# Layers written out one by one in a two-layer transformer step, with the seam between them ordered by token tile

## The reference, cut to what matters

```
for l in range(DEPTH):
    mod = silu(c) @ w_ada[l] + b_ada[l]             # sh1, sc1, g1, sh2, sc2, g2
    u = rmsnorm(h, norm1_g[l]) * (1 + sc1) + sh1
    proj = u @ w_in[l]                              # q, k, v, conv input, gates
    merged = sigmoid(gate_a) * attention_branch + sigmoid(gate_c) * conv_branch
    h = h + g1 * (merged @ w_out[l])
    u2 = rmsnorm(h, norm2_g[l]) * (1 + sc2) + sh2
    h = h + g2 * grouped_moe(u2)                    # 16 experts, two for each token
y = rmsnorm(h, final_norm_g)
```

## Time and profile before

| | us |
|---|---|
| median of 3 runs | 1873.3 (1868.39 to 1873.57) |
| profiled execution, its own time | 1872.31 |
| its span | 1870.7 |
| PE busy | 1565.5 (84%) |
| DVE busy | 1221.8 (65%) |
| ACT busy | 785.7 (42%) |
| POOL busy | 738.5 (39%) |

### The profile page before, as it was taken

The page is one execution under the profiler, slowest core; times in us unless marked ns, Lnnn a source line. Parts: engine busy times, 40 slices in busy tenths (PEclk is TensorE's granted clock), DMA queues, the critical chain, the costliest instruction groups (busy, mean ns, idle before and its releaser), DMA issues.

```text
span 1870.7 us, 27095 instructions
## 1 busy us (share of the span) xinstructions
PE 1565.5 (84%) x8954; PEld 1338.9 (72%) x8954; DVE 1221.8 (65%) x1662; ACT 785.7 (42%) x1178; POOL 738.5 (39%) x440
## 2 busy tenths in 40 slices
PE   2699899989998975999549989998999988499970
PEld 0589766679997764777438986666999967377750
DVE  0658588878937364777194947887886445477725
ACT  0422577752224132766142247776222413176621
POOL 2124399421114201887212329862111220179941
PEclk7799999999999976999869999999999989599995
DMA  7612165322212642999852205551222262479976
GB/s 289 200 45 68 53 208 203 99 58 80 68 57 91 247 156 110 342 356 338 314 187 74 68 30 181 188 163 36 68 69 78 80 247 83 178 281 353 379 268 235
DMA packets 131206, 310.06 MB, mean 166 GB/s; under 512 B 11636, under 2 KB 81396, under 8 KB 109984
## 3 DMA queue, kind: packets, MB, share of 16 engines
q1 hardware_dynamic: 104096, 224.41, 35.0%
q0 software_dynamic: 16400, 42.90, 6.1%
q10 hardware_dynamic: 10560, 40.90, 5.7%
HBM read 287.06 MB, written 39.44 MB: 175 GB/s over the span
## 4 chain that ended last, share of the span: by engine, by line
PE 62%; DMA 14%; DVE 11%; issue 7%; ACT 4%; POOL 1%; DVEq 0%; ACTq 0%; POOLq 0%; SPq 0%
PE ps L539 26%; PE ps L498 9%; PE ps L800 6%; PE ps L597 3%; PE ps L607 2%; DVE gu_lo L1498 2%; DMA raw_x<-in_w_down 2%; PE ps L454 2%; DMA raw<-in_w_down 2%; PE ps L866 2%; DMA raw<-in_w_up 2%; PE ps L586 2%; DMA raw<-in_w_ada 2%; PE ps L846 2%; PE ps L587 1%
## 5 line engine op out<-in xcount | busy, mean ns | idle before, releaser
L2279 POOL TENSOR_TENSOR w_lo<-raw,w_hi 128x1024 fp32r<-128x1024 f32 (+1 forms) x46 | 162.5, 3535 | 554.9 <-ACT w_hi L1106 554.9
L539 PE MATMUL ps<-u_hi,w_hi 128*128 128x320 f32 x768 | 238.9, 311 | 5.4 <-ACT probs L1205 5.4
L539 PE MATMUL ps<-u_lo,w_hi 128*128 128x320 f32 x768 | 238.1, 310 | 0.0
L539 PE MATMUL ps<-u_hi,w_lo 128*128 128x320 f32 x768 | 238.1, 310 | 0.0
L1106 ACT ACTIVATE w_hi<-raw 128x2048 fp32r<-128x2048 f32 (+1 forms) x64 | 101.3, 1591 | 293.7 <-PE ps L539 133.9
L1853 DVE SCALAR_TENSOR_TENSOR glu<-glu,convw 128x670 f32<-128x670 f32 x164 | 171.1, 1043 | 6.1 <-DVE o_lo L1808 0.6
L539 PEld LDWEIGHTS ps<-u_hi,w_hi 128*128 128x128 f32 x768 | 144.8, 189 | 6.0 <-ACT probs L1205 5.9
L539 PEld LDWEIGHTS ps<-u_lo,w_hi 128*128 128x128 f32 x768 | 144.8, 189 | 0.1
L539 PEld LDWEIGHTS ps<-u_hi,w_lo 128*128 128x128 f32 x768 | 144.8, 189 | 0.0
L2384 POOL DMA_INDIRECT xe<-u_d,tab_u x34 | 68.4, 2012 | 179.6 <-issue 145.2
L1713 DVE TENSOR_TENSOR pt_lo<-ps,pt_hi 128x512 fp32r<-128x512 f32 x160 | 109.7, 687 | 29.9 <-ACT pt_hi L1231 27.8
(11 more groups left out here) (379 smaller groups left out, 4254.2 us busy)
## 6 DMA issues: line engine op xcount, KB each, us to landing
raw<-in_w_ada SPq DMA_DIRECT2D x52, 1024.0 KB, 5.1
raw<-in_w_in SPq DMA_DIRECT2D x48, 512.0 KB, 5.0
raw_x<-in_w_gate SPq DMA_DIRECT2D x16, 1024.0 KB, 7.0
raw<-in_w_up SPq DMA_DIRECT2D x16, 1024.0 KB, 8.3
raw_x<-in_w_down SPq DMA_DIRECT2D x16, 1024.0 KB, 9.2
raw_x<-in_w_up SPq DMA_DIRECT2D x14, 1024.0 KB, 8.6
raw<-in_w_gate SPq DMA_DIRECT2D x14, 1024.0 KB, 6.5
raw<-in_w_down SPq DMA_DIRECT2D x14, 1024.0 KB, 9.2
```

Of the source, the lines that this page charges most:

```text
L539: ins = mm(ps[:, b, 0:HALF], (w_hi, w_lo)[w][:, s, cols(k):cols(k) + P], xs[x][:, k, half * HALF:(half + 1) * HALF], start=(k == 0 and w + ...
L2279: g_.tensor_tensor(w_lo[:, n % 2, 0:k], raw[:, n % 2, 0:k], w_hi[:, n % 2, 0:k].bitcast(F32), ALU.subtract).then_inc(*G.up("g_lo", "w_lo", n))
```

## The change

The five loops over layers become Python loops: each layer's instructions are written out, and every wait compares with a constant. What differs between the layers can then be left out of one of them.

- The results of layer 0 move to the head of layer 1. ACT issues the first three reads of `y_in` (`results_in`) in place of the five, and the other two from inside `squares`. DVE makes the result of tile t+1 (`result_before`) ahead of `u_lo_of(t)` and `um_of(t + 1)`, and `w_lo` of units 0 and 1 behind `um_of(0)` and `um_of(1)`; those of units 2 and 3 come after the last tile.
- ACT runs `squares(0)`, `squares(1)`, and then for each t `u_hi_of(t)`, `squares(t + 2)`, `q_of(0, t - 1)`. The squares write their unused output into `y_in`.
- PE transposes tile t+1 between the two halves of the projection of tile t.
- Each store of `h` has its own semaphore (`h_st0` to `h_st4`), and each copy of q waits for its own tile's store.
- Layer 0 runs the same new order without results.
- The last layer (`final`) leaves out group 0 of ada: eight loads, their matmuls, `modulation(0)`, `scale_row(0)`, `norm_rows`, `bias(0)`, `modulated_rows`; and the five stores of `h` with the wait for them at the end. Its results stay at its end.

```diff
@@ -470,14 +474,24 @@
         for name, by in (("ov_yfull", 1), ("ov_gu", 1), ("ov_xt", 1)):
             eng.sem_inc(sems(name), by)
         ledger.section = "layer"
-        with eng.Fori(0, DEPTH) as l:
+        last_drained, next_bank = dict(last), fills.at
+        for l in layers:
             T.l = l
+            last.clear()
+            last.update(last_drained)
+            fills.at = next_bank
+            final = l == DEPTH - 1
             def ada_of(u):
                 if not 0 <= u < N_ADA:
                     return
                 g, k = divmod(u, KC)
+                if final and MOD_ORDER[g] == 0:
+                    if k == 0:
+                        fill(("ada", 0), 7)
+                    eng.sem_inc(*(T.up("ada_used", "ada_used", 0, k) if k < KC - 1 else T.filled(("ada", 0))))
+                    return
                 ada(MOD_ORDER[g], k, raw_of(U_ADA + u), T.at("w_raw", U_ADA + u))
...
@@ -509,15 +523,14 @@
                     if kh == 0:
                         if t == NT - 1:
                             ins.then_inc(*T.up("w_used", "w_used", U_QKV))
+                        else:
+                            u_transposes(t + 1)
                     else:
                         ins.then_inc(*T.filled(("qkv", 0, t)))
             u_transposes(0)
-            u_transposes(1)
             for t in range(NT):
                 first_columns(t)
-                if t + 2 < NT:
-                    u_transposes(t + 2)
             for nu in range(1, 3):
                 bs = [fill(("qkv", nu, t)) for t in range(NT)]
                 for kh in range(2):
...
@@ -974,7 +988,7 @@
                     eng.wait_ge(*S.at("w_lo", N_UNITS - 3 + n, previous=True))
                     eng.wait_ge(*S.at("ada_used", "first", 4 + n))
                 elif n < U_MOE:
-                    eng.wait_ge(*S.at(*raw_free(n - 2)))
+                    eng.wait_ge(*S.at(*raw_free(n - 2 - KC if final and U_GATE <= n < U_GATE + 2 else n - 2)))
                     if n >= U_ADA + 2 * KC and n < U_GATE:
                         eng.sem_inc(sems("passed_S"), 1)
                 elif n < U_MOE + 2:
...
@@ -1000,7 +1014,9 @@
                           for i, c0 in enumerate((GA0, GB0))))
             for u in range(N_ADA):
                 g, k = divmod(u, KC)
-                of = l if MOD_ORDER[g] else DEPTH - 1 - l
+                if final and MOD_ORDER[g] == 0:
+                    continue
+                of = l if MOD_ORDER[g] else l + 1
                 c0 = MOD_ORDER[g] * MODW
                 load(U_ADA + u, (raw_of(U_ADA + u), io["w_ada"][of, k * P:(k + 1) * P, c0:c0 + MODW]))
             for b8 in range(KC):
...
@@ -1110,15 +1127,26 @@
                 act(expert_half(n, 1), expert_raw(n), ACT.Copy).then_inc(*A.up("a_hi", "w_hi", n))
+            def results_in(t):
+                A.l = l - 1
+                eng.dma_start(y_in[:, t % 3, :, :], y_rows[t]).then_inc(*A.up(f"y_in{t}", "y_in", t, by=16))
+                A.l = l
+
+            def squares(t):
+                eng.wait_ge(*A.at("h", t, previous=True))
+                if t >= 3:
+                    eng.wait_ge(*A.at("ss1", t - 3))
+                act(y_in[:, t % 3, 1, :], h_cur[:, t, :], ACT.Square, accum_out=ssq[:, t:t + 1]).then_inc(*A.up("a_ss", "ss1", t))
+                eng.wait_ge(*A.at("ss1", t))
+                if l and t + 3 < NT:
+                    results_in(t + 3)
+                act(std[:, t:t + 1], ssq[:, t:t + 1], ACT.Sqrt, bias=eps[:, :], scale=1.0 / D).then_inc(*A.up("a_ss", "std1", t))
+
+            if l:
+                for t in range(3):
+                    results_in(t)
             for n in range(U_QKV, U_QKV + 2):
                 hi(n)
-            for t in range(NT):
-                eng.wait_ge(*A.at("h", t, previous=True))
-                if t:
-                    eng.wait_ge(*A.at("ss1", t - 1))
-                act(junk1[:, :], h_cur[:, t, :], ACT.Square, accum_out=ssq[:, t:t + 1]).then_inc(*A.up("a_ss", "ss1", t))
-                eng.wait_ge(*A.at("ss1", t))
-                act(std[:, t:t + 1], ssq[:, t:t + 1], ACT.Sqrt, bias=eps[:, :], scale=1.0 / D).then_inc(*A.up("a_ss", "std1", t))
             def u_hi_of(t):
                 b = A.bank(("uT", t, 0))
...
@@ -1131,19 +1159,19 @@
                 b = A.bank(("qkv", nu, t))
                 act(q_tok[:, t, nu * 512:(nu + 1) * 512], ps[:, b, :], ACT.Copy).then_inc(*A.drained(("qkv", nu, t)))
-            u_hi_of(0)
-            u_hi_of(1)
-            hi(U_QKV + 2)
+            squares(0)
+            squares(1)
+            for t in range(NT):
+                u_hi_of(t)
+                if t + 2 < NT:
+                    squares(t + 2)
+                if t >= 1:
+                    eng.wait_ge(*A.at("h_stored", t - 1, previous=True))
+                    q_of(0, t - 1)
+                if t >= 3:
+                    hi(U_QKV + t - 1)
             eng.wait_ge(*A.at("h_stored", NT - 1, previous=True))
-            q_of(0, 0)
-            u_hi_of(2)
-            hi(U_QKV + 3)
-            q_of(0, 1)
-            u_hi_of(3)
-            q_of(0, 2)
-            u_hi_of(4)
-            q_of(0, 3)
-            q_of(0, 4)
+            q_of(0, NT - 1)
             hi(U_QKV + 4)
             hi(U_QKV + 5)
             for t in range(NT):
...
@@ -1442,10 +1470,10 @@
             eng.wait_ge(*A.at("y_sent", NE - 1))
             eng.wait_ge(sems("ov_sent"), 16 * (o0 + n_over) + 16)
             eng.wait_ge(sems("ov_xts"), o0 + n_over + 1)
-            for t in range(NT):
+            for t in range(NT) if final or not ledger.known else ():
                 if t >= 3:
                     eng.wait_ge(*A.at("h", t - 3))
-                eng.dma_start(y_in[:, t % 3, :, :], y_d.rearrange("(x t p) d -> t p x d", p=P, x=2)[t]).then_inc(*A.up(f"y_in{t}", "y_in", t, by=16))
+                eng.dma_start(y_in[:, t % 3, :, :], y_rows[t]).then_inc(*A.up(f"y_in{t}", "y_in", t, by=16))
     @block.vector
...
@@ -1489,7 +1520,6 @@
                 if n < U_MOE:
                     if n == U_QKV:
                         eng.wait_ge(*V.at("arow", "first"))
-                        eng.wait_ge(*V.at("h", NT - 1, previous=True))
                     if n == U_QKV + 1:
                         eng.wait_ge(*V.at("mod_out", "first"))
                     k = size(n)
...
@@ -1505,8 +1535,6 @@
                 eng.wait_ge(*V.at("v", V.steps))
                 if t == 0:
                     eng.wait_ge(*V.at("rows1_in", previous=True))
-                if t == 1:
-                    eng.wait_ge(*V.at("ss1", NT - 1))
                 if t >= 2:
                     eng.wait_ge(*V.at("filled", ("uT", t - 2, 1)))
                 v.scalar_tensor_tensor(out=um[:, t % 2, :], in0=h_cur[:, t, :], scalar=rstd[:, t:t + 1], in1=rows1[:, t // LT, 1, :],
...
@@ -1523,20 +1551,39 @@
                 ALIAS(("drained", ("uT", t, 1)), ("drained", ("uT", t, 0)))
                 ALIAS(("u_lo", t), ("drained", ("uT", t, 0)))
+            def result_of(t, of):
+                V.l = of
+                y = y_in[:, t % 3, :, :]
+                if t == 0:
+                    eng.wait_ge(*V.at("g2_in", 1))
+                    eng.wait_ge(*V.at("ha_in"))
+                eng.wait_ge(*V.at("y_in", t))
+                v.tensor_tensor(y[:, 0, :], y[:, 0, :], y[:, 1, :], ALU.add).then_inc(*V.up("v_y", "y_sum", t))
+                eng.wait_ge(*V.at("y_sum", t))
+                v.tensor_tensor(y[:, 0, :], y[:, 0, :], g2_row[:, t // LT, :], ALU.mult).then_inc(*V.up("v_y", "y_gated", t))
+                eng.wait_ge(*V.at("y_gated", t))
+                v.tensor_tensor(h_cur[:, t, :], ha_in[:, t, :], y[:, 0, :], ALU.add).then_inc(*V.up("v_h", "h", t))
+                V.l = l
+
+            def result_before(t):
+                if l:
+                    result_of(t, l - 1)
+
+            result_before(0)
+            result_before(1)
+            um_of(0)
             lo(U_QKV)
-            um_of(0)
+            u_lo_of(0)
             um_of(1)
-            u_lo_of(0)
             lo(U_QKV + 1)
-            u_lo_of(1)
-            um_of(2)
-            um_of(3)
+            for t in range(1, NT):
+                if t + 1 < NT:
+                    result_before(t + 1)
+                u_lo_of(t)
+                if t + 1 < NT:
+                    um_of(t + 1)
             lo(U_QKV + 2)
-            u_lo_of(2)
-            um_of(4)
-            u_lo_of(3)
             lo(U_QKV + 3)
-            u_lo_of(4)
             eng.wait_ge(*V.at("small_loaded"))
             for x in range(2):
...
@@ -1799,9 +1846,12 @@
                 inverse(h // 2)
                 maxima(h + 3, 0)
                 probs_lo(h + 2, 0)
-                if h in (2, 6, 10):
+                if h in (2, 6) or h == 10 and not final:
                     modulation(MOD_ORDER[h // 4])
-                if h == 12:
+                if h == 10 and final:
+                    eng.wait_ge(*V.at("filled", ("ada", 0)))
```

(34 more changed lines are left out.)

24 lines of the change are left out of this document (10 added, 14 removed).

## The result

The changed kernel takes 1856.84 us (median of 4 runs, 1856.49 to 1859.23) against 1873.1 us before: ratio 0.9922, interval 0.9908 to 0.9936. The medians lie 16.3 us apart, the ratio makes it 14.6 (12.0 to 17.2), where 11.4 were forecast. On a second chip it was 1853.08 against 1872.59, ratio 0.9896 (0.9877 to 0.9916), or 19.5 us. The profiled run took 1856.78 us, its span 1855.0, 15.7 less than before.

What follows compares the result with a forecast made beforehand. TensorE's matrix work, 62% of the chain, was taken to bound the kernel. Terms 0 + 1.2 - 3.3 - 6.8 - 2.5 = -11.4 us from 1872.3 gave 1860.9, as median 1861.9; range 1848 to 1869.

Steps and rivals of the forecast that it cites:

- The seam: Between layers: first projection 15.5 us earlier, given back by the last tile; booked 0, at most 1.4 us gained.
- a turn of 10.7: Tile loop at the seam: DVE and ACT steps that cannot overlap take 10.7 us per tile, against TensorE's 6.3.
- Rival (a): Tile loop at the seam overlaps better, DVE's own work bounds it at 7.5 us a turn; 1852 us, chance 0.12.
- Rival (b): TensorE's clock stays low through the tile loop, 12.2 us a tile, seam ends 12 us later; 1874 us, chance 0.08.
- The head of layer 0: Start of the first layer: new order without results delays transposes and keeps the clock low longer; loss 1.2 us (0.9 to 3).
- The last layer's units: Last layer's attention: dropping eight unused ada units shortens two pairs of heads; gain 3.3 us, bounds 1.3 and 8.5.
- The tail: End of the last layer: without stores of h, fin_row lands before DVE wants it; gain 6.8 us, bounds 6.0 and 7.
- Waits on constants: Whole chain: wait thresholds become constants once the loop is gone; gain 2.5 us, bounds 0 and 10.7.
- A quarter: Share of the chain's 10.7 us of queue pieces booked as gain, 2.5 us, since most stand in the attention stage.
- Rival (c): Whole chain: waits and register work are worth all of their 10.7 us; 1854 us, chance 0.10.
- rival (d): Fetching twice the straight code stops engines, 3.00 us a stop; six slow the kernel 0.3%, ten give 1891; chance 0.05.

Runs made afterwards that it cites:

- s1: Changed kernel with one ACT line moved: squares of tile t+1, not t+2, come behind u_hi of tile t, from tile 2 on; 1847.39 us, ratio 0.9872.
- a1: Changed kernel with the last layer's eight 1 MB loads of unused modulation weights put back, without their matmuls; 1859.49 us.
- a2: Changed kernel with the last layer's 32 matmuls of the unused modulation put back, without their loads; 1859.68 us.
- e3: Kernel of e1, with the last layer's stores of h also left out; 1857.06 us.
- e1: Kernel before the change with only its five layer loops written out, old order at the seam and nothing left out; 1859.79 us, ratio 0.9936.

## Why the prediction was right, and where it was not

**The seam: right, in each step.** First projection nearer by 15.5 us in the forecast, 15.7 in the trace; a turn of 10.7, measured 10.5; TensorE idle about 4.3, measured 3.9 (the 1.49 before 966.49 is short because the tile before it ran half at the low clock); the end at 0 to 1.4 us earlier, measured 0.35. What the forecast's frame hid is that it set the new order against a kernel that also pays for its loop. Against the old order written out, the new one loses 1.3 to 3.4 us. The 15 us that meet the eye are a shift of work, not a saving: the five results are still done by the same engine before the last tile's modulated row.

**Rival (a), a turn of 7.5,** did not come, by the order of lines alone; s1 gives 7.94 with it mended, 0.4 of which is the squares' root that my 7.5 left out.

**Rival (b), the clock.** In the profile above the matmul at 956.02 and the eleven behind it run at the low level, 0.43 us apart, after 3.88 us of idling. By tile, the granted clock is 0.78, 0.76, 1.00 and 0.79 in this profile and 0.76, 0.84, 0.84 and 0.80 in the second one of the same kernel; yet the seam takes 61.25 and 61.26. The rule of the Trainium skill that idle gaps bring the clock down (TensorE: Matmul & The Clock Gate, Why this matters for your kernels) agrees with the rows, but here the turn is set by DVE and ACT, and what the clock takes in the first tiles is covered by TensorE's idle time. At the tile before the last one it is not, as its first half stands ahead of the last tile's transposes. In a1, whose seam is the same, that whole half ran at the low level behind 3.91 us of idling:

```profile
978.79:983.90 5.11, 5.11 (x12) 0.50 0.09 17
```

There the last u_lo comes 0.8 us later than in the profile above, and the seam takes 62.1 us (61.9 in a2). The forecast had named this place, with a loss of 1.7 us. It had also misread a row: it took the 32 matmuls behind 3.64 us of idling in the earlier trace rows for the high level. Their granted clock is 0.81 as a whole, full for the first microsecond and then

```profile
909.40:910.40 1.00, 1.00 (x4) 0.50 0.94 389
```

so both of its idle stretches were followed by the low level.

**The head of layer 0: sign wrong.** The part I worked out is there: from the first transposes to the end of the three blocks 91.4 to 92.4 us in four profiles against 89.7 to 90.8 in eight, so +1.6 by the means where I had 1.2. What I did not see is in front of it: the first transposes start at 58.0 to 59.3 us in the six profiles with the new order and at 60.4 to 62.2 in the eight with the old one. Their rows wait for the modulation's way through memory, and w_lo(0) now stands behind um(0), so the slot of the first weights is not free and SyncE's next load is not issued. SyncE's queue in the kernel with the old order and everything else, and in the changed one (each line stands for two loads and spans the time from the first issue to the second):

```profile
45.41 23.07 SPq L1001 DMA_DIRECT2D raw<-in_w_in  x2
```

```profile
61.42 7.42 SPq L1001 DMA_DIRECT2D raw<-in_w_in  x2
```

The stretch from mod_d's store on (all engines' busy times; the clock, the DMA share and GB/s stand last), before and after:

```profile
43.50:50.00 6.50, 0.00 (x0) 0.00 (x0) 2.64 (x2) 2.85 (x3) 2.79 (x6) 0.50 0.35 48
```

```profile
43.50:50.00 6.50, 0.00 (x0) 0.00 (x0) 0.00 (x0) 1.56 (x1) 1.82 (x4) 0.50 0.02 5
```

0.35 of the DMA engines were busy beside the modulation's small transfers and 0.02 are now; um starts at 55.5 to 56.7 in the four profiles with this head, against 57.8 to 58.9 in the old order written out. That the empty queues are the cause is argued from these rows; no run moved w_lo alone. Net, by the means of four and eight profiles, -0.7 instead of +1.2. The step that failed is the one that priced w_lo(0) at its new place and did not look at who waits for its slot.

**The last layer's units: right.** Forecast 22.1 and 18.1 for the two pairs, measured 21.73 and 18.19: 3.5 us less than in the earlier trace rows, 3.1 less than in the kernel of e3, which has the units but no loops; the pair behind them gains another 0.5 against that kernel. The matmuls alone bring back 2.7 of these 3.1 (a2), the loads nothing (a1), as the sum had it.

**The tail: right, and then a loss.** 6.8 forecast, 6.8 measured (30.9 to 24.0; 0.8 of it belongs to the constants, by the loops alone). But behind the last xn the end comes 2.3 us later. The trace shows where: the last output has landed, and then GpSimd's queue closes the program with a DRAIN instruction. Before and after:

```profile
L161 POOLq DRAIN  x1: 6855/6855/6855, 1863.7 to 1863.7; - x1
```

```profile
L163 POOLq DRAIN  x1: 9060/9060/9060, 1845.7 to 1845.7; - x1
```

It takes 6.86 us in the kernels with everything kept, 6.45 with the stores left out, 6.20 with the units left out, and 9.06 in all seven kernels or profiles with both left out, a1 and a2 among them, so neither the loads nor the matmuls of the units decide it. Why this instruction is longer there stays open.

**Waits on constants: the term that was mis-sized.** Forecast 2.5, bounds 0 and 10.7; the loops alone are worth 12 (8 to 16). 2 of it are the loop's way back at the seam, which in my sum could not count. My upper bound added only the pieces that the chain calls queue time (10.7 us, 4.3 in e1). The short issue pieces around them fell by a further 9.7 us, and the chain's issue time as a whole by over 50. Outside the seam the loops gave 10 us (6 to 15), so the bound of 10.7 is not clearly broken, but the pieces it summed fell by only 6.4: they do not account for the gain, and no sum of pieces does. A quarter was too little, and the argument that TensorE's full queue would hide most did not hold: attention, where I put the cover, gained 0.9 us in layer 0 and 2.4 in layer 1 (means of the two profiles of before and of e1 and e3). Rival (c) was nearer in this term than the forecast, though not for the reason it gave, as only 6.4 of its 10.7 us of pieces went. Of rival (d), stops for code, the chain shows no new one: its longest issue pieces are the same two in both kernels, 4.35 us before and 4.5 after.

**The sum.** By stages of the first two profiles: seam -0.4, head -0.8, units -3.5, tail -6.8, end +2.3; what is left of the -15.7 is -6.5 for the constants outside the seam and for chance. This rest can't be split by profiles: 3.0 of it are the first layer's experts (152.7 against 149.7), and with the second profiles of both kernels it runs from -9.8 to +1.3. What holds for the constants is e1's 8 to 16 us. The forecast of -11.4 came within 3 to 8 us of the two chips' results, and that is in part luck. The constants gave some 9 us more than I had, and the cost of the new order against the old one (2.3 at the seam) and the longer DRAIN at the end (2.3) took about half of that back.

## What to carry to other kernels

When work moves from a block into a loop of tiles, write down the order of each engine and add up what cannot overlap: a gain of 15 us at the first tile was worth nothing at the last, and one line moved on the idle engine was then worth 9. Compare the new order with the old one under the same other edits; here writing out the loops alone gave most of the gain, and the new order took some of it back. When waits lose their registers, don't bound the gain by one kind of piece in the chain: the queue pieces fell by 6 us, the issue pieces by over 50, and the kernel by 12; a run with the loops alone written out settles it. Before a small rest is given a cause by subtracting stages, profile each kernel twice. Before moving an instruction that frees a slot, ask which transfer waits for that slot and what runs beside it.

## What the runs showed of the hardware

A wait against a register costs 0.12 us between two dependent instructions on VectorE, one against a constant 0.02. A VectorE addition of 1.22 us with both inputs in SBUF takes 3.25 when GpSimd adds beside it (2.9 to 3.3 us), since it waits for all of it; one that began first kept its 1.28. Eight 1 MB loads at 202 to 211 GB/s beside a TensorE stage cost 0.0 us. TensorE's clock was at the 1.2 GHz level behind the idle stretches of 3.6 to 3.9 us shown here, at once or up to 1.3 us after the work began again. The DRAIN that ends GpSimd's queue took 6.2 to 9.1 us with nothing else running.
